# A fused encoder layer with expert retrieval: the residual stream is turned for the queries as it is, and the norm's root is applied to the query as it leaves PSUM

## The reference, cut to what matters

```python
h = h + concatenate([y_a, y_b, y_c]) @ w_out
u = rmsnorm(h, ffn_norm)                   # h * rsqrt(mean(h*h) + eps) * gain
q = (u @ w_query).reshape(s, 8, 2, 128)    # 8 heads, two halves
sc = einsum("shtd,htkd->shtk", q, sub_keys)          # 128 keys per half
top_s, top_i = top_k(sc, 16)               # 16 + 16, their 256 sums, the best 16
idx, gates = ...                           # 8 * 16 = 128 experts per token
act = gelu(einsum("td,ted->te", u, peer_u[idx])) * gates
h = h + einsum("te,ted->td", act, peer_v[idx])
```

## Time and profile before

| | us |
|---|---|
| median of 3 runs | 3279.82 |
| lowest and highest | 3279.13, 3282.3 |
| span of the profiled execution, first to last instruction | 3274.6 |
| first gather of `peer_u` issued | 280.54 |
| first gather of `peer_v` issued | 360.60 |

### The profile page before, as it was taken

The page is one execution under the profiler, slowest core; times in us unless marked ns, Lnnn a source line. Parts: engine busy times, 40 slices in busy tenths (PEclk is TensorE's granted clock), DMA queues, the critical chain, the costliest instruction groups (busy, mean ns, idle before and its releaser), DMA issues.

```text
span 3274.6 us, 34131 instructions
## 1 busy us (share of the span) xinstructions
PE 2383.7 (73%) x11010; PEld 1162.2 (35%) x11010; DVE 2178.8 (67%) x5274; ACT 867.7 (26%) x2209; POOL 1967.3 (60%) x2064
## 2 busy tenths in 40 slices
PE   8998987877888778668778868767765545555546
PEld 4754445533343545333333545333321111111111
DVE  1346777877566787686666778696656777777750
ACT  3452433342132332331232223341111111111100
POOL 0002565666566667676566657676667777777764
PEclk9999988898999887869899878878887677777668
DMA  5345999999999999999999999999999999999996
GB/s 196 133 181 189 400 420 420 386 420 403 421 420 421 420 419 412 420 393 420 420 420 421 403 414 402 420 416 420 421 420 419 419 419 419 419 419 419 420 411 240
DMA packets 332296, 1267.10 MB, mean 387 GB/s; under 512 B 37288, under 2 KB 43600, under 8 KB 313432
## 3 DMA queue, kind: packets, MB, share of 16 engines
q0 software_dynamic: 294912, 1073.87, 80.9%
q1 hardware_dynamic: 37208, 191.04, 14.6%
HBM read 1256.22 MB, written 12.09 MB: 387 GB/s over the span
## 4 chain that ended last, share of the span: by engine, by line
DMA 34%; PE 29%; POOL 19%; DVE 9%; issue 8%; ACT 1%; POOLq 0%; DVEq 0%; SPq 0%; ACTq 0%
DMA v_ring<-peer_v,idx_v 22%; POOL v_ring L1068 8%; DMA u_ring<-peer_u,idx_u 8%; POOL u_ring L1054 8%; PE ps L2382 7%; PE ps L2072 6%; DVE u_ring L1877 4%; DMA front<-peer_u,idx_u 3%; PE ps L2206 2%; PE ps L2302 2%; PE ps L2315 2%; POOL front L1068 1%; POOL front L1054 1%; PE ps L2288 1%; PE ps L2087 1%
## 5 line engine op out<-in xcount | busy, mean ns | idle before, releaser
L1877 DVE CUSTOM_DVE_ANT_0 u_ring<-u_ring,ps 128x1024 f32<-128x1024 f32 x920 | 1107.0, 1217 | 520.4 <-DMA u_ring<-peer_u,idx_u 513.0
L1054 POOL DMA_INDIRECT u_ring<-peer_u,idx_u x920 | 881.9, 959 | 670.6 <-DVE idx_u L1849 275.1
L1068 POOL DMA_INDIRECT v_ring<-peer_v,idx_v x924 | 885.6, 958 | 531.6 <-PE ps L2382 278.3
L2382 PE MATMUL ps<-v_ring,spread 128*32 128x512 f32 x3696 | 700.9, 830 | 658.3 <-DMA v_ring<-peer_v,idx_v 577.7
L2382 PEld LDWEIGHTS ps<-v_ring,spread 128*32 128x32 f32 x3696 | 140.6, 134 | 972.1 <-issue 970.2
L2072 PE MATMUL ps<-front 128*128 128x512 f32 x864 | 384.7, 601 | 0.0
L2072 PEld LDWEIGHTS ps<-front 128*128 128x128 f32 x864 | 162.6, 192 | 220.5 <-issue 220.1
L2382 PE MATMUL ps<-front,spread 128*32 128x512 f32 x400 | 135.9, 913 | 113.0 <-DMA v_ring<-peer_v,idx_v 90.3
L2206 PE MATMUL ps<-front 128*128 128x256 f32 x768 | 189.3, 402 | 5.6 <-DVE soft L1699 5.6
L1877 DVE CUSTOM_DVE_ANT_0 front<-front,ps 128x1024 f32<-128x1024 f32 x104 | 126.5, 1219 | 73.4 <-DMA front<-peer_u,idx_u 71.7
L2206 PEld LDWEIGHTS ps<-front 128*128 128x128 f32 x768 | 150.8, 202 | 62.5 <-issue 41.6
(11 more groups left out here) (278 smaller groups left out, 3268.0 us busy)
## 6 DMA issues: line engine op xcount, KB each, us to landing
front<-weight_blocks SPq DMA_DIRECT2D x135, 1024.0 KB, 7.7
v_ring<-peer_v,idx_v POOLq DMA_INDIRECT x924, 14.2
u_ring<-peer_u,idx_u POOLq DMA_INDIRECT x920, 14.1
front<-x SPq DMA_DIRECT2D x14, 512.0 KB, 8.6
front<-c_bias_all SPq DMA_DIRECT2D x32, 192.0 KB, 5.9
front<-keys_turned SPq DMA_DIRECT2D x4, 1024.0 KB, 12.2
v_ring<-weight_blocks SPq DMA_DIRECT2D x4, 1024.0 KB, 5.5
front<-ple_w_gate SPq DMA_DIRECT2D x1, 4096.0 KB, 23.1
```

The lines of the kernel that those rows point to most:

```text
L1054: nc.gpsimd.indirect_dma_start(row, None, io["peer_u"][0], bass.IndirectOffsetOnAxis(ap=k.idx_u[:, t % 2, j:j + 1], axis=0)).then_inc(here ...
L1068: nc.gpsimd.indirect_dma_start(row, None, io["peer_v"][0], bass.IndirectOffsetOnAxis(ap=k.idx_v[:, m % 2, column:column + 1], axis=0)).the ...
L1877: nc.vector.tensor_tensor_reduce(out=row, in0=row, in1=k.un_ps, scale=1.0, scalar=0.0, op0=ALU.mult, op1=ALU.add, accum_out=k.dots[:, t % ...
L2382: last = mm(k.acc_ps[32 * j:32 * j + 32, half * 512:(half + 1) * 512], centres[:, at:at + 32], row[:, half * 512:(half + 1) * 512], start= ...
```

## The change

PE transposes the residual stream itself, so `n2_t` waits for the residual sum of its own half (`o_add` of that half) and no more. The gain is multiplied in when the transposes leave PSUM: by DVE for tile 0, in one multiply for each half, and by ACT for all other tiles, in four scaled copies for each half. The reciprocal root is multiplied in by ACT when it copies a query unit from PSUM (`scaled_query`), which waits for it. `un` and its multiply are gone; its place holds the queries and the squares. `n2` on DVE is the reciprocal alone. The first half of a query unit waits for the first half of the transposes only. Orders change: in group 0 the first half of tile 0's transposes stands ahead of the last output block, the first query half right behind that block, then the second half of the transposes, the root and the turns of y, and tile 1's next output block behind the query's second half. In tile 1, and in the later groups, the transposes stand ahead of `n2`; there `hold` now stands between the `n2` of the two tiles. SP stores an odd tile's stream when both its halves are summed. One more row of gains (`ffn_gain`) is among the constants, and `by_scalar` sends `n2_t` of tile 0 to DVE. Below is the diff without the lists of names, the semaphores and the dispatch.

```diff
...
@@ -214,7 +214,8 @@
         if g and u == 0:
             first, second = ([("p1", t, u, half) for half in range(2)] for t in tiles_of(g))
-            out += turned_norm(g * GT) + first[:1] + [("o_add", g * GT + 1, 1), ("n2", g * GT + 1, 1)] + turned_norm(g * GT + 1) + second[:1] + [("hold", g * GT)] + first[1:] + second[1:]
+            even, odd = tiles_of(g)
+            out += first[:1] + [("n2_t", even, 1), ("n2", even, 1), ("o_add", odd, 1)] + second[:1] + [("n2_t", odd, 1), ("hold", even), ("n2", odd, 1)] + first[1:] + second[1:]
         else:
...
@@ -245,12 +246,13 @@
         out += first[1:4] + second[:1] + first[4:6] + o[:1] + first[6:] + [("z_silu", g)] + gates[:1]
         out += second[1:4] + [("b_n", 0, 1)] + second[4:6] + o[1:2] + second[6:] + gates[1:] + [("b_n", 1, 1)]
-        out += turned[0] + own_o(0) + [("n2", 0, 1)]
+        blocks, halves = own_o(0), turned_norm(0)
+        out += turned[0] + blocks[:6] + halves[:1] + blocks[6:]
     else:
         out += silu + bias + c + [("y_n", g)] + z + first[:SEG_PARTS] + mixed + first[SEG_PARTS:] + second + [("z_silu", g)] + gates + [("b_n", g * GT, GT)]
         out += o[:2] + turned[0] + turned[1] + o[2:5] + [("o_add", t, 0) for t in tiles_of(g)] + o[5:]
         first, second = (own_o(t) for t in tiles_of(g))
-        out += first + second[:1] + [("o_add", g * GT, 1), ("n2", g * GT, 1)] + second[1:]
+        out += first + [("n2_t", t, 0) for t in tiles_of(g)] + second[:1] + [("o_add", g * GT, 1)] + second[1:]
     return out
...
@@ -268,8 +270,8 @@
     second, second_keys = query_of(0, 1)
     tops = [[("top", k, i) for i in range(6)] for k in range(2)]
-    out = [("y_t", "b", 1, half) for half in range(2)] + own_o(1, (1, 0)) + turned_norm(0)
-    out += first + [("un", 0)] + first_keys + tops[0] + [("g_exp", 0)] + tops[1] + [("g_norm", 0)]
+    out = first[:1] + turned_norm(0)[1:] + [("n2", 0, 1)] + [("y_t", "b", 1, half) for half in range(2)]
+    out += first[1:] + [("un", 0)] + own_o(1, (1, 0)) + first_keys + tops[0] + [("g_exp", 0)] + tops[1] + [("g_norm", 0)]
     out += own_o(1, (1, 1), (0, 2)) + second[:1] + own_o(1, (0, 3)) + second[1:]
...
@@ -278,7 +280,7 @@
     first, first_keys = query_of(1, 0)
     second, second_keys = query_of(1, 1)
-    return [own_o(1, (1, 3)), [("n2", 1, 1)] + turned_norm(1) + first, first_keys[:1] + second[:1] + first_keys[1:],
+    return [own_o(1, (1, 3)), turned_norm(1) + [("n2", 1, 1)] + first, first_keys[:1] + second[:1] + first_keys[1:],
             second[1:], second_keys]
...
@@ -400,7 +402,7 @@
 def by_scalar(kind, t):
-    return t < LAST if kind == "g_t" else t >= GT
+    return t < LAST if kind == "g_t" else t >= (1 if kind == "n2_t" else GT)
...
@@ -517,7 +519,7 @@
         elif kind in singles:
             t = at[1] if kind == "y_t" else at[0]
-            plan.take(step, pool, 1, 4 if kind in ("n1_t", "y_t", "g_t") and by_scalar(kind, t) else singles[kind])
+            plan.take(step, pool, 1, 4 if kind in ("n1_t", "y_t", "n2_t", "g_t") and by_scalar(kind, t) else singles[kind])
         if n < BEHIND:
...
@@ -613,7 +615,6 @@
         self.pT_c = in_yT(1280, 1024).rearrange("p (b k n) -> p b k n", b=2, n=P)
         self.c_bias = in_yT(2304, 1280).rearrange("p (b n) -> p b n", n=C_KEYS)
-        self.q = in_yT(0, 1024).rearrange("p (b n) -> p b n", n=UNIT)
...
@@ -638,7 +639,8 @@
         self.skT = arena(0, 2048).rearrange("p (h k) -> p h k", k=PK)
-        self.un = arena(2048, 2048).rearrange("p (t n) -> p t n", n=D)
+        self.q = arena(2048, 1024).rearrange("p (b n) -> p b n", n=UNIT)
+        self.squared = arena(2048, 2048).rearrange("p (t n) -> p t n", n=D)
         self.h = arena(4096, 2048).rearrange("p (t n) -> p t n", n=D)
...
@@ -902,7 +904,8 @@
     def keep_tiles(g):
         for t in filter(through_hbm, tiles_of(g)):
-            sp.wait_ge(k.un_full, t + 1)
+            for c in range(2):
+                copied(("o", g, c, t % GT))
             sp.dma_start(rows(k.stream, t), k.h_of(t)).then_inc(k.h_out, 16)
...
@@ -1147,12 +1150,17 @@
                 act_fn(k.cn[:, "kq".index(unit[1]), lt, :], ps, ACT.Copy).then_inc(copied_, 1)
             else:
-                act_fn(k.q[:, lt, :], ps, ACT.Copy).then_inc(copied_, 1)
+                scaled_query(t, ps, copied_)
+
+    def scaled_query(t, ps, copied_):
+
+        act.wait_ge(k.n2_rs, t + 1)
+        act_fn(k.q[:, t % GT, :], ps, ACT.Copy, scale=k.rs[:, t:t + 1]).then_inc(copied_, 1)
     def first_query(t, u, half):
         if half:
             _, ps, copied_ = filled(("p", t // GT, f"q{u}", t % GT))
-            act_fn(k.q[:, t % GT, :], ps, ACT.Copy).then_inc(copied_, 1)
+            scaled_query(t, ps, copied_)
...
@@ -1339,7 +1347,7 @@
             copied(("o", g, 1, lt))
         for i in range(t, t + n):
-            chain.link(act_fn(k.un[:, i % GT, :], k.h_of(i), ACT.Square, accum_out=k.rs[:, i:i + 1]))
+            chain.link(act_fn(k.squared[:, i % GT, :], k.h_of(i), ACT.Square, accum_out=k.rs[:, i:i + 1]))
         root(k.rs[:, t:t + n], D).then_inc(k.n2_root, 1)
...
@@ -1347,11 +1355,6 @@
         act.wait_ge(k.after_out, 16 * (t - 1))
         act_fn(k.tile_io[:, t % 2, :], k.h_of(t), ACT.Copy).then_inc(k.tile_held, 1)
-
-    def n2_t(t, half):
-        _, ps, copied_ = filled(("n2_t", t, half))
-        lt = t % GT
-        act_fn(k.uT[:, 4 * half:4 * half + 4, lt * P:(lt + 1) * P], ps.rearrange("p (c n) -> p c n", n=P), ACT.Copy).then_inc(copied_, 1)
...
@@ -1394,6 +1397,10 @@
         four = slice(4 * half, 4 * half + 4)
         copy_scaled(("n1_t", t, half), k.uT[:, four, t % GT * P:(t % GT + 1) * P], k.mix_gain[:, four])
+
+    def n2_t(t, half):
+        four = slice(4 * half, 4 * half + 4)
+        copy_scaled(("n2_t", t, half), k.uT[:, four, t % GT * P:(t % GT + 1) * P], k.ffn_gain[:, four])
...
@@ -1788,15 +1795,13 @@
     def n2(t, n):
-
-        g = t // GT
-        if t == 0:
-            dve.wait_ge(k.row_gain_in, 16)
         inverse(k.n2_root, t + 1, k.rs[:, t:t + n], k.n2_rs)
-        dve.wait_ge(k.n2_rs, t + 1)
-        for lt in range(t % GT, t % GT + n):
-            stt(k.un[:, lt, :], k.h_of(g * GT + lt), k.rs[:, g * GT + lt:g * GT + lt + 1], k.gain_row[:], ALU.mult, ALU.mult).then_inc(k.un_full, 1)
-
+
+    def n2_t(t, half):
+        _, ps, copied_ = filled(("n2_t", t, half))
+        lt, four = t % GT, slice(4 * half, 4 * half + 4)
+        tt(k.uT[:, four, lt * P:(lt + 1) * P], ps.rearrange("p (c n) -> p c n", n=P),
+           k.ffn_gain[:, four].unsqueeze(2).broadcast_to([P, 4, P]), ALU.mult).then_inc(copied_, 1)
...
@@ -1864,8 +1869,10 @@
             dve.wait_ge(k.u_free, t * KK)
         else:
+            dve.wait_ge(k.row_gain_in, 16)
             for place, count in k.un_before:
                 dve.wait_ge(k.copied[place], count)
+        dve.wait_ge(k.n2_rs, t + 1)
         stt(k.un_ps, k.tile_io[:, t % 2, :], k.rs[:, t:t + 1], k.gain_row[:], ALU.mult, ALU.mult).then_inc(k.un_kept, 1)
...
@@ -2077,9 +2086,8 @@
     def first_query(t, u, half):
         w = block(t // GT, U_Q + 2 * u + half)
+        copied(("n2_t", t, half))
         if half == 0:
-            for part in range(2):
-                copied(("n2_t", t, part))
             ps, filled = open_(("p", t // GT, f"q{u}", t % GT))
...
@@ -2319,11 +2327,11 @@
     def n2_t(t, half):
-        pe.wait_ge(k.un_full, t + 1)
+        copied(("o", t // GT, half, t % GT))
         ps, filled = open_(("n2_t", t, half))
         for c in range(4):
             at = (4 * half + c) * P
-            last = turn(ps[:, c * P:(c + 1) * P], k.un[:, t % GT, at:at + P], ident)
+            last = turn(ps[:, c * P:(c + 1) * P], k.h_of(t)[:, at:at + P], ident)
         last.then_inc(filled, 1)
...
```

More of the change, by code:

```diff
@@ L66 @@
 KEPT_BLOCKS = (U_O + 4, U_O + 5, U_O + 6, U_O + 7, U_Q + 1)
-CONSTS = dict(mix_gain=DCH, out_gain=16, ple_gain=DCH, qk_gain=4, sink=A_HEADS, rows=3 * B_HEADS, taps=XCH * B_CONV, conv_bias=XCH,
+CONSTS = dict(mix_gain=DCH, ffn_gain=DCH, out_gain=16, ple_gain=DCH, qk_gain=4, sink=A_HEADS, rows=3 * B_HEADS, taps=XCH * B_CONV, conv_bias=XCH,
               dt_weights=DCH * B_HEADS)
@@ L566, in __init__ @@
         self.consts = sb("consts", [P, sum(CONSTS.values())])
-        self.mix_gain, self.out_gain, self.ple_gain, self.qk_gain, self.sink, rows, taps, self.conv_bias, wdt = self.const_parts()
+        self.mix_gain, self.ffn_gain, self.out_gain, self.ple_gain, self.qk_gain, self.sink, rows, taps, self.conv_bias, wdt = self.const_parts()
         self.rows = rows.rearrange("p (j h) -> p j h", h=B_HEADS)
@@ L1508, in scalar_program @@
             n2(*at)
-        elif kind == "n2_t":
+        elif kind == "n2_t" and by_scalar("n2_t", at[0]):
             n2_t(*at)
@@ L1988, in vector_program @@
             n2(*at)
+        elif kind == "n2_t" and not by_scalar("n2_t", at[0]):
+            n2_t(*at)
         elif kind == "top":
```

6 lines of the change are left out of this document (3 added, 3 removed).

## The result

| | median us | lowest to highest | runs |
|---|---|---|---|
| before | 3281.06 | 3279.13 to 3284.19 | 4 |
| after | 3341.78 | 3338.32 to 3343.84 | 4 |

What follows compares the result with a forecast made beforehand. DMA bytes were taken to bound 85% of the span, so only the stretch before the engines are full could gain: 1.8 + 3.8 - 0.6 + 2.0 = 7.0 us, 3279.8 to 3272.8 us. Range 3268.0 to 3278.5; own case 5 to 9.5 us gain.

Steps and rivals of the forecast that it cites:

- Groups 1 to 3: Later tile groups, constants load and stream stores: no bytes touched, counted as zero, with +-1.5 us for other alignment.
- rival (2): From 280 to 370 us both DMA holes close, and later queries' PE stops shorten: 10.5 us gained, 3269.3 us; chance 0.13.
- Part 1: Tile 0: first query turned at 265.3 us instead of 267.03, 1.8 us earlier, bounds 1.0 and 2.0.
- (a): Start of the gathers: tile 0's earlier query lets the DMA queues start earlier, worth +1.8 us.
- Part 2: Tile 1: query starts 2.0 us after its last output block instead of 7.9, putting PE 8.7 us further ahead.
- half-clock price: Tile 1's first eight query matmuls: 6.19 us at the slow clock instead of 3.60, 2.6 us of PE's lead.
- (b): 300 to 322 us: PE's lead of 10.5 us brings query-weight loads forward into the hole, worth 3.8 us, between nothing and 5.0.
- (d): 350 to 370 us: v indices copied earlier, POOL's 5.09 us idle goes, worth 2.0 us, bounds 1.0 and 3.5.
- (c): 322 to 350 us: tile 0's dots lead by 0.9 us instead of 1.8, worth -0.6 us.
- (1): Tile 0's start and the hole at 360 us: only these gain, PE's lead is swallowed; 2.5 us, 3277.3 us; chance 0.20.
- (3): Tile 0's first query isn't earlier, from a late weight block or PSUM wait: 4 us gain, 3275.8 us; chance 0.07.
- (4): Later groups: ACT's row-buffer copy waits for a store, DMA runs dry; 30 us wait costs 13, 3286 us; chance 0.04.

Runs made afterwards that it cites:

- e1: The changed kernel with the unused tile edge cut from 24 to 16 columns, so u_ring is at 8192 again: 3272.8 us, ratio 0.9972 of the kernel before.
- e6: The changed kernel with u_ring at 8192 and tile 1's query again behind the root, tile 0's part kept: 3455.3 us, ratio 0.9994, on a slower chip.
- e15: The changed kernel with u_ring at 8192 and tile 1's query again behind the root, repeated on another slower chip: 3478.4 us, ratio 0.9997.
- e2: The kernel before with edge at 32 columns instead of 24, so u_ring and all behind it lie 32 bytes higher: 3347.3 us, ratio 1.0204.
- e9: The kernel before with u_ring and all tiles behind it 32 bytes higher, run again on another chip: 3346.95 us, ratio 1.0201.
- e8: The changed kernel with u_ring at 8192 and DVE's reciprocal of tile 1 one slot later: 3451.7 us, ratio 0.9990, on a slower chip.
- e16: The changed kernel with u_ring at 8192 and tile 0's query in its old order, tile 1's part kept: 3475.6 us, ratio 0.9993, on a slower chip.
- e18: The kernel before with v_ring and four of u_ring's seven buffers 32 bytes off, repeated on a slower chip: 3464.8 us, ratio 1.0020.

## Why the prediction was wrong

The step that failed is one sentence under "Groups 1 to 3": **"A row of gains adds 4 KB to a 140 KB load at the start: nothing."** The load does cost nothing. But the row also has a place in the SBUF, in a tile that stands ahead of both rings and of the weight ring, and its 32 bytes moved every buffer of the three off its boundary. The same paragraph says "Nothing of it touches bytes", and the last one expects "416 GB/s, 2800 us long, as before". With 85% of the span bound by those bytes, 2% of the packet time was 65 us, against a sum of 7.0 for all other terms. No rival had it, and neither end of the range. The profile of before could not show it by a row, for no gather and no block of the weight ring is off the boundary in it; but the step could have been seen open: the argument itself says that only bytes per microsecond count after 380 us, so each edit had to be asked what it does to the transfers, their addresses included. The trace of before has the other hint, 99% of the gathers' packets from 400 to 600 us at the same 159 ns.

The rest can be read in e1, where the address is put right.

- **The sum.** 7.0 us forecast; 9.0 measured in e1 (3281.79 to 3272.8), within the 5 to 9.5 of its own case; by its interval it is 5.6 to 12.8, so the time alone can't tell 7.0 from the 10.5 of rival (2). That e1 is 3272.8 to the decimal is chance: its chip had the kernel before 2 us higher. The profiled span was to be about 3267.6 and is 3268.2.
- **Part 1, (a).** First query turned at 265.3 forecast, 264.97 measured; first gather 278.7 forecast, 278.43 measured. That holds for the early place of the first gather; the changed kernel's own profile has 270.58 and 284.04, with more of PE's time at 1.2 GHz ahead of it, which the prediction had no term for. PE in order of time in e1, 256 to 305 us:

```profile
256.56 0.60 PE L2334 MATMUL ps<-ident,tile_io 128*128 128x128 f32 x4
...
258.03 3.67 PE L2095 MATMUL ps<-v_ring,front 128*128 128x512 f32 x8
...
264.97 0.60 PE L2341 MATMUL ps<-ident,front 128*128 128x128 f32 x4
...
293.62 0.60 PE L2334 MATMUL ps<-ident,tile_io 128*128 128x128 f32 x4
294.57 0.66 PE L2334 MATMUL ps<-ident,tile_io 128*128 128x128 f32 x4 [0.35 <-DVE tile_io L1795]
295.50 3.67 PE L2095 MATMUL ps<-front 128*128 128x512 f32 x8 [0.27 <-issue]
299.01 3.60 PE L2095 MATMUL ps<-v_ring,front 128*128 128x512 f32 x8
303.38 0.65 PE L2341 MATMUL ps<-ident,front 128*128 128x128 f32 x4 [0.78 <-ACT front L1158]
```

- **Part 2.** Output block done at 293.62, query from 295.50: X+1.9, where X+2.0 was forecast. The matmuls take 3.67 us and not 6.19, so the upper level of the clock (2.4 GHz, granted 1.00 from 300 to 322) was kept; PE idles only 0.35 and 0.27 us ahead of them, against the 5.09 and 0.89 of the earlier trace rows. In e6, with the root's wait back, PE idles 3.77 and 0.43 us ahead of them and the same eight take 5.09 us. Over all traces the granted clock of 300 to 322 us is 0.77 to 0.84 where tile 1 has its old order, 0.93 and 0.94 in e6 and e15, and 1.00 wherever tile 1 has the new one. The half-clock price of 2.6 us (2.5 measured) and its cause were right.
- **ACT and DVE.** Eight scaled copies took 2.17 us against 2 x 1.06; the squares, the table load and the root follow at once, in e1:

```profile
294.26 2.17 ACT L1395 ACTIVATE front<-ps,consts 128x128 f32<-128x128 f32 x8 [2.99 <-PE ps L2334]
296.27 1.10 ACT L1350 ACTIVATE front<-tile_io 128x1024 f32<-128x1024 f32 x1
...
297.48 1.28 ACT L1099 ACT_TABLE_LOAD   x1
298.78 0.29 ACT L1099 ACTIVATE rs<-rs,eps 128x1 f32<-128x1 f32 x1
```

The reciprocal follows at 299.10, after an idle of 3.11 us, and dot 2 at 299.18, where 299.8 was forecast and 300.76 was before.
- **The holes, (b) to (d).** Against 420 GB/s e1 loses 20 x (1 - 288/420) = 6.3 us, then 3.4, 0.9 and 0.05: 10.6 where the earlier trace rows gave 19.3. Of the 8.7 won, 1.3 lie in 280 to 300 (where (a) had 1.8, part of it ahead of 280), 4.1 in 300 to 322, where (b) had 3.8, -0.1 in 322 to 350, where (c) had -0.6, and **3.4** in 350 to 370, where (d) had 2.0. Term (d) was mis-sized: I left 1.5 us for latency of gathers under way, and the hole closed wholly, at 419 GB/s. The v gathers start at 352.11 and not at 354.9, because the u gather ahead of them came at 350.87 and not at 353.7. That is 8.5 us ahead of before, where 5.7 were forecast.
- **Rivals**, in e1. (1), only the start counts, is out: 300 to 322 moves 356 GB/s. (2), both holes close, holds for the second; the first still loses 3.4 us. (3) is out: the first query is turned at 264.97. (4), slower through `hold`, had the right sign with the wrong mechanism: the last store that the copy waits for is issued at 2324.5 and the copy runs at 2368.8 in the changed kernel, 44.3 us of margin (39.7 in e1) where before had 46.

Putting the rings back is worth 69 us in the changed kernel (3341.8 to 3272.8, in two sets of runs) and 65 in the kernel before (e2, e9). By their intervals, about 0.2% or 5 us to either side, the two can't be told apart.

The version to keep is e1: 0.9972 [0.9961, 0.9983] of before, and 2.1% under the change as it was made.

## What to carry to other kernels

In a stretch that is bound by bytes, ask of every edit what it does to the transfers, and of every tile that grows what lies behind it: print the SBUF addresses of the transfer targets before and after, and compare them modulo 256. Compare the rate of the full stretch first (416 against 407 GB/s at the same DMA share) and then the time of one packet; they tell a slower transfer from a new wait at once. A tile that nothing reads may be padding that holds an address.

## What the runs showed of the hardware

- Gathers of 4096-byte rows whose places in SBUF are 32 or 64 bytes off a multiple of 256 take a median of 162 ns, not 159, and 65 or 61 us of 3282; 256 bytes off cost nothing.
- The cost isn't a sum over packets: one ring off, 45% of all rows (920 or 924 of 2048 gathers), gave 5 to 6 us; all rows and the weights gave 65.
- The front of the kernel before ends 3 to 5 us earlier or later from one trace to the next, and that goes with PE's granted clock: with 20 us at 1.2 GHz between 90 and 245 us the first gather comes near 280.3, with 24 to 27 us between 283.2 and 285.6.
- Sets of runs on different chips differ more than all of this. In three of them the kernel before took 3281 to 3282 us, in three others 3458, 3481 and 3462. The traces of the latter with every row on the boundary (e6 to e8, e15, e16) have the same median packet of 159 ns but a mean of 165.5 to 166.5, and 388 to 393 GB/s in place of 416 over 380 to 3180 us. There the 32 bytes cost 0.4 to 0.5% (both rings); all tiles off, which cost 2.0% on the others, wasn't run there. No chip of e1 to e18 was used for two sets, so whether it is the chip or what else went on at the time isn't shown.
